# Gate matrices in a transformer block on one Trainium2 core: two products of rounded one-hots in place of one fp32 product, key constants in PSUM, and a contiguous copy of the experts' gate column

## What is computed

```python
q = (xt @ w_q).reshape(T, PEER_HEADS, 2, PEER_HALF)
s = jnp.einsum('thpc,hpnc->thpn', q, sub_keys)
s_top, i_top = lax.top_k(s, PEER_TOPK)
...
best_s, pos = lax.top_k(cand_s, PEER_TOPK)
idx = jnp.take_along_axis(cand_i, pos, axis=-1)
gate = jax.nn.softmax(best_s.astype(jnp.float32), axis=-1).astype(xn.dtype)
...
    act = jax.nn.gelu(jnp.einsum('tkd,td->tk', u_tab[ib], xb), approximate=False)
    return jnp.einsum('tk,tkd->td', act * gb, v_tab[ib])
```

## Time and profile before

| | us |
|---|---|
| median of 3 runs | 1575.96 |
| lowest and highest of the runs | 1575.76, 1586.25 |
| span of the profiled execution | 1581.1 |
| PE busy, DVE busy, ACT busy in that span | 1524.7, 1326.5, 720.5 |
| mean granted TensorE clock | 0.992 of full speed |

### The profile page before, as it was taken

The page is one execution under the profiler, slowest core; times in us unless marked ns, Lnnn a source line. Parts: engine busy times, 40 slices in busy tenths (PEclk is TensorE's granted clock), DMA queues, the critical chain, the costliest instruction groups (busy, mean ns, idle before and its releaser), DMA issues. The chain is left out here.

```text
span 1581.1 us, 24984 instructions
## 1 busy us (share of the span) xinstructions
PE 1524.7 (96%) x9451; PEld 1388.1 (88%) x9451; DVE 1326.5 (84%) x2360; ACT 720.5 (46%) x1442; POOL 339.2 (21%) x301
## 2 busy tenths in 40 slices
PE   7999799999999999999998999999999999999999
PEld 6898688889998999989998999999999888888887
DVE  4638777776799999988974999998989999999996
ACT  4553454141344698788763333333333334333332
POOL 4011620010466100301220222222322211111100
PEclk9999899999999999999999999999999999999999
DMA  5220004031444567878998999999998999999982
GB/s 197 86 81 1 8 29 160 30 111 50 132 165 153 168 196 214 316 241 282 366 366 312 334 360 354 341 352 328 372 339 315 354 407 376 380 363 340 351 290 97
DMA packets 152236, 384.12 MB, mean 243 GB/s; under 512 B 11072, under 2 KB 92096, under 8 KB 135488
## 3 DMA queue, kind: packets, MB, share of 16 engines
q1 hardware_dynamic: 122176, 232.75, 41.9%
q0 software_dynamic: 18432, 134.23, 23.4%
q10 hardware_dynamic: 11520, 15.73, 2.7%
HBM read 337.58 MB, written 45.09 MB: 242 GB/s over the span
## 5 line engine op out<-in xcount | busy, mean ns | idle before, releaser
L1795 POOL DMA_INDIRECT scores<-in_peer_uv,pair_index x86 | 126.2, 1468 | 620.2 <-DVE pair_sum L1819 503.2
L1984 PE MATMUL bank<-x_hi,u_split 128*128 128x384 f32 x640 | 220.3, 344 | 10.6 <-POOL u_split L1919 5.5
L1986 PE MATMUL bank<-x_hi,u_split 128*128 128x384 f32 x640 | 215.8, 337 | 0.0
L1985 PE MATMUL bank<-x_lo,u_split 128*128 128x384 f32 x640 | 215.6, 337 | 0.0
L2273 PE MATMUL bank<-v_hi,act_hi 128*128 128x512 f32 x528 | 206.2, 391 | 1.0 <-DVE v_lo L2336 1.0
L2275 PE MATMUL bank<-v_hi,act_lo 128*128 128x512 f32 x528 | 205.9, 390 | 0.0
L2274 PE MATMUL bank<-v_lo,act_hi 128*128 128x512 f32 x528 | 205.7, 390 | 0.0
L2352 DVE TENSOR_TENSOR act_tile<-gelu_tile,onehots 128x384 f32<-128x384 f32 x128 | 118.2, 923 | 43.8 <-ACT gelu_tile L2321 33.1
L2310 ACT ACTIVATE act_hi<-act_tile 128x384 fp32r<-128x384 f32 x128 | 66.6, 521 | 182.0 <-PE bank L2275 130.9
L1984 PEld LDWEIGHTS bank<-x_hi,u_split 128*128 128x128 f32 x640 | 121.0, 189 | 13.0 <-issue 5.9
L2261 PE MATMUL bank<-x_hi,u_split 128*128 128x384 f32 x384 | 129.1, 336 | 1.4 <-PEq L1929 1.4
(11 more groups left out here) (325 smaller groups left out, 3625.0 us busy)
## 6 DMA issues: line engine op xcount, KB each, us to landing
v_raw<-in_peer_v SPq DMA_DIRECT2D x128, 512.0 KB
u_raw<-in_peer_u SPq DMA_DIRECT2D x64, 512.0 KB, 7.0
u_raw_more<-in_peer_u SPq DMA_DIRECT2D x64, 512.0 KB, 6.7
gates<-gate_stage SPq DMA_DIRECT2D x24, 1024.0 KB, 6.0
onehots<-gates SPq DMA_DIRECT2D x32, 768.0 KB, 8.9
early_gelus<-early_gelu ACTq DMA_DIRECT2D x80, 192.0 KB
gelu_tile<-early_gelus SPq DMA_DIRECT2D x80, 192.0 KB
w_raw<-in_w_in SPq DMA_DIRECT2D x9, 1024.0 KB, 5.2
```

What stands on the lines that cost most here:

```text
L1795: pool.indirect_dma_start(self.slot(k), None, self.table, bass.IndirectOffsetOnAxis(ap=self.sidx[:, k:k + 1], axis=0)).then_inc(self.lande ...
L1984: nc.tensor.matmul(banks.bank(g)[:, 0:TD], uh[:, q, w], m.xh[:, k, P:], start=(k == 0), stop=False)
L1985: nc.tensor.matmul(banks.bank(g)[:, 0:TD], uh[:, q, w], m.xl[:, k, P:], start=False, stop=False)
L1986: t = nc.tensor.matmul(banks.bank(g)[:, 0:TD], ul[:, q, w], m.xh[:, k, P:], start=False, stop=(k == KD - 1))
```

## The change

Four edits, in `Selection`, `routing` and `experts`.

1. The plain one-hots `oj` and the gated ones `og` become fp32r tiles, and each token's gate matrix is the sum of two products: `og`, whose scale is the gate and which is rounded on the way out, and a new tile `ogl`, whose scale is the gate minus its rounded value (`smallT[:, :, 3]`, made once per block by two small DVE instructions). ACT builds both, so `gated` issues 16 instructions a batch. The rings become 2 (`oi`, `og`, `ogl`) and 3 (`oj`).
2. `iota`, `row0` and `step` move to PSUM bank 7, by `place_constants`. The routing stage hands out 7 banks.
3. In `experts` ACT first copies the gate column to a contiguous `act_tile` (`copy_gate`), of which there are now two, and DVE multiplies the gelu into it in place.
4. `load_gates` waits for the copies in place of the multiplications.

```diff
@@ class Selection
-        self.iota = mem.take("rt_iota_row", [P, NK])
+        self.iota_made = mem.take("rt_iota_row", [P, NK])
...
-        self.step = part_of("index_steps", [P, 2, PH, TOPK])
...
+    def place_constants(self, dve, bank):
+
+        link = self.link(dve)
+        self.iota, self.row0 = bank[:, 0:NK], bank[:, NK:NK + TOPK]
+        self.step = bank[:, 256:512].rearrange("p (q h a) -> p q h a", q=2, h=PH)
+        link(self.nc.vector.tensor_copy(self.iota, self.iota_made[:]))
+        link(self.nc.vector.tensor_copy(self.row0, self.row0_made[:]))
@@ def routing
+    og_lo_ready = sem("rt_onehot_gated_low")
+    banks = Banks(ps[:7], done, {"act": sem("rt_by_act"), "dve": sem("rt_by_dve")})
...
-    RING = 3
+    RI, RJ, RG = 2, 3, 2
...
-        oj = m.mem.over("onehot_j", [P, RING, BT, NK], "onehots")
-        oi = m.mem.over("onehot_i", [P, RING, BT, NK], "onehots", F32, 4 * RING * BT * NK)
-        og = sb("onehot_gated", [P, RING, BT, NK])
-        smallT = sb("rt_smallT", [P, 2, 3, P])
+        oj = m.mem.over("onehot_j", [P, RJ, BT, NK], "onehots", F32R)
+        oi = m.mem.over("onehot_i", [P, RI, BT, NK], "onehots", F32, 4 * RJ * BT * NK)
+        og = sb("onehot_gated", [P, RG, BT, NK], F32R)
+        ogl = [m.mem.over("onehot_gated_low0", [P, BT, NK], "onehots", F32R, 4 * (RJ + RI) * BT * NK),
+               sb("onehot_gated_low1", [P, BT, NK], F32R)]
+        smallT = sb("rt_smallT", [P, 2, 4, P])
...
+                        pe.wait_ge(og_lo_ready, BT // 4 * n + i + 1)
                         for q in range(4):
-                            t = nc.tensor.matmul(banks.bank(g)[:, q * NK:(q + 1) * NK],
-                                                 og[:, slot(b, k), 4 * i + q, :], oj[:, slot(b, k), 4 * i + q, :],
-                                                 start=True, stop=True)
+                            out, t = banks.bank(g)[:, q * NK:(q + 1) * NK], 4 * i + q
+                            nc.tensor.matmul(out, og[:, n % RG, t, :], oj[:, n % RJ, t, :], start=True, stop=False)
+                            t = nc.tensor.matmul(out, ogl[n % RG][:, t, :], oj[:, n % RJ, t, :], start=False, stop=True)
...
                     act.wait_ge(oi_ready, n + 1)
-                    wait_products(act, n)
+                    wait_products(act, n - RG)
                     for t in range(BT):
-                        ins = nc.scalar.activation(og[:, slot(b, k), t, :], oi[:, slot(b, k), t, :], ACT.Copy,
+                        ins = nc.scalar.activation(og[:, n % RG, t, :], oi[:, n % RI, t, :], ACT.Copy,
                                                    scale=smallT[:, b % 2, 1, k * BT + t:k * BT + t + 1])
+                        low = nc.scalar.activation(ogl[n % RG][:, t, :], oi[:, n % RI, t, :], ACT.Copy,
+                                                   scale=smallT[:, b % 2, 3, k * BT + t:k * BT + t + 1])
...
                     banks.wait_taken(dve, ("small", b))
+                    link = sel.link(dve)
+                    link(nc.vector.tensor_copy(gate_hi[:], smallT[:, b % 2, 1]))
+                    link(nc.vector.tensor_tensor(smallT[:, b % 2, 3], smallT[:, b % 2, 1], gate_hi[:].bitcast(F32),
+                                                 ALU.subtract))
...
                 early_low(0)
+                sel.place_constants(dve, ps[7])
@@ def experts
-        af = m.mem.over("act_tile", [P, TD], "early_gelu")
+        af = [m.mem.over("act_tile0", [P, TD], "early_gelu"), m.mem.take("act_tile1", [P, TD], at_end=True)]
...
+                def copy_gate(n):
+                    it, jj = n // BODY, n % BODY
+                    if jj == 0:
+                        act.wait_ge(g_in[it % 2], 32 * (it // 2 + 1))
+                    if n >= 2:
+                        act.wait_ge(gated, n - 1)
+                    else:
+                        act.wait_ge(nxt.ge_out[n], 16 * (EARLY // 2))
+                    nc.scalar.activation(af[n % 2][:], gt[:, it % 2, :, jj], ACT.Copy).then_inc(gate_cols, 1)
+
                 split_u(1)
+                copy_gate(0)
...
+                    if n + 1 < NK:
+                        copy_gate(n + 1)
                     if n + 2 < NMT:
                         split_u(n + 2)
...
-                    nc.vector.tensor_tensor(af[:], ge[n % NG2][:], gt[:, it % 2, :, jj], ALU.mult).then_inc(gate_f, 1)
+                    dve.wait_ge(gate_cols, n + 1)
+                    nc.vector.tensor_tensor(af[n % 2][:], ge[n % NG2][:], af[n % 2][:], ALU.mult).then_inc(gate_f, 1)
```

More of the change, by code:

```diff
@@ L1332, in __init__ @@
         self.zsum = part_of("rt_z", [P, PH])
-        self.row0 = part_of("row_starts", [P, TOPK])
+        self.row0_made = part_of("row_starts", [P, TOPK])
         self.rowd = part_of("row_lengths", [P, TOPK])
@@ L1861, in routing @@
     stored = [sem("gates_out0"), sem("gates_out1")]
-    banks = Banks(ps, done, {"act": sem("rt_by_act"), "dve": sem("rt_by_dve")})
+    og_lo_ready = sem("rt_onehot_gated_low")
+    banks = Banks(ps[:7], done, {"act": sem("rt_by_act"), "dve": sem("rt_by_dve")})
     BT = 8
     NBT = P // BT
-    RING = 3
+    RI, RJ, RG = 2, 3, 2
     ST = 16
@@ L1908, in routing @@
         stage = sb("gate_stage", [P, 2, NK // GJ, ST, GJ])
-        oj = m.mem.over("onehot_j", [P, RING, BT, NK], "onehots")
-        oi = m.mem.over("onehot_i", [P, RING, BT, NK], "onehots", F32, 4 * RING * BT * NK)
-        og = sb("onehot_gated", [P, RING, BT, NK])
-        smallT = sb("rt_smallT", [P, 2, 3, P])
-        small, iota = sel.small, sel.iota
+        oj = m.mem.over("onehot_j", [P, RJ, BT, NK], "onehots", F32R)
[4 more added lines that the diff above has]
+        smallT = sb("rt_smallT", [P, 2, 4, P])
+        gate_hi = sb("rt_gate_hi", [P, P], F32R)
+        small = sel.small
         u_raw = m.u_raw
@@ L1919, in u_low @@
             return on.tensor_tensor(ul[:, n % 2, :], u_raw[n % NU], uh[:, n % 2, :].bitcast(F32), ALU.subtract)
-        def slot(b, k):
-            return (NBT * (b - 1) + k) % RING
         def wait_products(eng, n):
-            if n >= RING:
-                banks.wait_full(eng, ("G",) + BATCHES[n - RING] + (BT // 4 - 1,))
+            if n >= 0:
+                banks.wait_full(eng, ("G",) + BATCHES[n] + (BT // 4 - 1,))
         with nc.Block() as block:
@@ L1996, in pairs @@
                     t.then_inc(done, 1)
-                keep_turning(nc, m, banks.banks[7], 18)
+                keep_turning(nc, m, banks.banks[6], 18)
                 for n in range(FIRST):
@@ L2102, in one_hot @@
                     return nc.vector.tensor_tensor(
-                        out[:, slot(b, k)], iota[:].unsqueeze(1).broadcast_to([P, BT, NK]),
+                        out, sel.iota.unsqueeze(1).broadcast_to([P, BT, NK]),
                         smallT[:, b % 2, q, k * BT:(k + 1) * BT].unsqueeze(2).broadcast_to([P, BT, NK]), ALU.is_equal)
@@ L2114, in first_keys @@
                 def first_keys(n):
-                    if n >= RING:
-                        dve.wait_ge(og_ready, BT // 4 * (n - RING + 1))
-                    one_hot(oi, n, 0).then_inc(oi_ready, 1)
+                    if n >= RI:
+                        dve.wait_ge(og_ready, BT // 4 * (n - RI + 1))
+                        dve.wait_ge(og_lo_ready, BT // 4 * (n - RI + 1))
+                    one_hot(oi[:, n % RI], n, 0).then_inc(oi_ready, 1)
                 early_low(0)
+                sel.place_constants(dve, ps[7])
                 sel.link(dve)(nc.vector.memset(pairs_of_0.sums[:], 0.0))
@@ L2131, in _ @@
                         first_keys(n + 1)
-                    wait_products(dve, n)
-                    one_hot(oj, n, 2).then_inc(oj_ready, 1)
+                    wait_products(dve, n - RJ)
+                    one_hot(oj[:, n % RJ], n, 2).then_inc(oj_ready, 1)
                     early_low(early(n) + 1)
@@ L2203, in load_gates @@
                     if it >= 2:
-                        sp.wait_ge(gate_f, (it - 1) * BODY)
+                        sp.wait_ge(gate_cols, (it - 1) * BODY)
                     v = slice(half * TD // 2, (half + 1) * TD // 2)
@@ L2309, in split_act @@
                         act.wait_ge(down_done, n - NA + 1)
-                    nc.scalar.activation(ah[:, n % NA, :], af[:], ACT.Copy).then_inc(gate_hi, 1)
+                    nc.scalar.activation(ah[:, n % NA, :], af[n % 2][:], ACT.Copy).then_inc(gate_hi, 1)
+                def copy_gate(n):
[7 more added lines that the diff above has]
+                    nc.scalar.activation(af[n % 2][:], gt[:, it % 2, :, jj], ACT.Copy).then_inc(gate_cols, 1)
                 split_u(1)
+                copy_gate(0)
                 for n in range(NK + 1):
@@ L2343, in gate @@
                         dve.wait_ge(ge_in[n % NG2], 16 * ((n - NMT) // NG2 + 1))
-                    it, jj = n // BODY, n % BODY
-                    if jj == 0:
-                        dve.wait_ge(g_in[it % 2], 32 * (it // 2 + 1))
-                    if n:
-                        dve.wait_ge(gated, n)
```

(8 more changed lines are left out.)

11 lines of the change are left out of this document (7 added, 4 removed).

## The result

The kernel after takes 1727.3 us (median of three runs, 1727.1 to 1729.1), before 1575.96. The ratio is 1.0949, with an interval of 1.0917 to 1.0981: slower by 151 us, where the forecast was 116 and its range ended at +144.

The account below looks back on a forecast made before the run. PE was taken to set the pace everywhere before the change. Routing +64.5 us, last part +47.5 and mixed part +4 summed to +116 on the 1576 us median, 1692 us; range 1655 to 1720.

Parts of the forecast that it names:

- constants in PSUM: Before the batches: PE's waits for POOL's work on u go, as DVE collides less with it; -5.5 us, bounds 0 and 5.5.
- batches: Gate batches: ACT's eight extra instructions make rounds 7.51 us in place of 5.16; 367 us against 294, +73 us.
- behind the batches: After the last batch: PE's 3.05 us wait for a low part of u goes, as DMAs have more room; -3 us.
- mixed part: Mixed part: rounds of 8.41 us against PE's 8.25 over 46 iterations, 7 us at most; +4 us taken.
- last part: Last part: rounds of 4.76 us against PE's 4.13; 377.8 us against 330.3, +47.5 us.
- The bounds on the fp32r product: Gate batches: an fp32r product of 128 columns costs PE between 0.06 and 0.224 us; 0.112 taken.
- D: Experts: time of ACT's strided copy of one gate column; 0.84 us taken, 0.52 if the stride costs nothing.
- the signs of being wrong: PE above 97% busy in either stretch, a copy under 0.6 us, or batch rounds under 7.3 or over 7.8 us.
- the forecast's own average: Mixed part: the round between ACT and DVE averages 7.57 us plus the copy's time, 8.41 against PE's 8.25.
- the closed round: Experts: `act_lo`, copy, `v_hi`, `v_lo`, pair step, next `act_lo`, without PE; 4.76 us in the last part against PE's 4.13.
- 25 us lower: Experts: how much the sum falls if ACT's strided copy runs at one element per cycle, whatever the stride.
- the rival's +86.5: Experts: rival in which ACT reads the gate column at full speed, 0.52 us; +86.5 us, 1662 us, chance 0.17.

Follow-up runs that it names:

- second profile of before: The unchanged kernel before, profiled once more to check the first profile's span; its span is 1574.9 us, 6.2 less, and its median 1576.6 us.
- psum_and_copy_behind: The kernel before with the selection's constants in PSUM, seven routing banks, and the experts' gate copy placed behind `v_hi`; no second one-hot; 1571.0 us, ratio 0.9956.
- Three_tiles: The kernel after with three `act_tile` in turn, so the copy waits for `act_lo` of n-2 in place of n-1; 1651.3 us, ratio 1.0458.
- copy_contiguous: The kernel after with ACT's copy reading 384 contiguous elements in place of every eighth, so the gates are wrong numbers; 1675.2 us, ratio 1.0616.
- copy_behind: The kernel after with the gate copy moved behind `split_v(n - 1)` in ACT's order, nothing left out; 1646.2 us, ratio 1.0433.

## Why the prediction was right and wrong

Against the second profile of before, the 152.5 us between the ends divide like this:

| step | forecast | measured |
|---|---|---|
| constants in PSUM | -5.5 | -7.2 |
| batches | +73 | +79.3 |
| behind the batches | -3 | -1.1 |
| mixed part | +4 | +21.3 |
| last part | +47.5 | +60.3 |

**Right.** ACT's in-order queue sets the batches, at 7.5 us per round as forecast. The copy closes a round between ACT and DVE in which PE has no part. Both halves were shown: without the eight low copies the 79 us of the batches go, and with the copy behind `v_hi`, or with a third tile, the last part returns to PE's 326 us. The bounds on the fp32r product were wide, and the value taken, 0.112 us, is what the rows show; the reason given for it (weights as many and as wide) was not tested, so that is in part luck. That DVE's saved 0.37 us per column are worth nothing is shown by psum_and_copy_behind.

**Wrong: D.** "I take 0.84, as DVE's is the only strided read of this very tile" is the step that failed. ACT's strided copy takes 0.97 us. I had charged the stride with ACT's own 0.82 ns per element once more, 0.32 us; it costs ACT 0.45 (DVE 0.37, which would have been too little as well). D stands in every round, so in the last part 79 x 0.13 = 10 us are from it, and about 6 in the mixed part. I gave the range an end below 0.84 and none above, and so it was with the signs of being wrong: none of them came true (PE 87 and 89% busy, a copy over 0.6 us, rounds of 7.5 us). D alone would have taken the forecast to about 1708 us, so it isn't the whole miss.

**Wrong: the mixed part.** "46 iterations give 7 us at most; PE has some room at the start, so I take 4." It cost 21.3. With D = 0.97 the forecast's own average is 7.57 + 0.97 = 8.54 against PE's 8.25. Measured, 44 rounds are 8.57 us and cost 13.9 us in all; so the closed round is right here too, and PE had no room that took anything off. The other 7.5 us, which the sum didn't have, lie at the two ends. PE's waits in after, before the first down and at the passage to the last part:

```profile
929.81 0.47 PE L2293 MATMUL bank<-v_hi,act_hi 128*128 128x512 f32 x1 [1.51 <-DVE v_lo L2369]
...
1321.35 0.47 PE L2293 MATMUL bank<-v_hi,act_hi 128*128 128x512 f32 x1 [1.98 <-DVE v_lo L2369]
...
1328.64 0.47 PE L2293 MATMUL bank<-v_hi,act_hi 128*128 128x512 f32 x1 [2.92 <-DVE v_lo L2369]
```

The first costs 1.7 us: the fourth up comes 10.03 us after the third, for 8.36 before. From the last up to column 48 it is 23.5 us for 17.7, which is 5.8: the waits ahead of columns 46 and 47 are 3.9 us longer in all than before, and behind the wait of 2.92 the down of column 47 runs at a lower granted clock, 5.8 us for 4.16. Three_tiles loses 1.7 and 3.1 us at the same places, 1.6 of them by the clock again, copy_contiguous 0.7 and 2.6, copy_behind nothing. So both come with the copy's place ahead of `v_hi`. I read it as the two places where PE has no columns in hand; no run isolates that. Rounds with four pair steps in place of three cost nothing by themselves: copy_contiguous has them, and its ups stay 8.25 us apart.

**Wrong: a column.** The row at 1244.23 is the down of column 47, not 48: in that profile `v_hi_late` is first read at 1248.4. The 330.3 us were 81 columns, 4.08 us each, and the forecast set 80 against them. That is 4 us.

**Wrong: the batches' edges, and one wait.** The sum had 48 rounds of 7.51 us. The first, which has nothing to evict yet, takes 4.69, and the last takes 10.6, from 884.64 to the end; the two nearly cancel. The larger part is one wait of ACT of 4.2 us, which its own round doesn't have:

```profile
666.99 16.48 SPq L1945 DMA_DIRECT2D u_raw<-in_peer_u  x1
...
690.38 1.06 ACT L2039 ACTIVATE u_split<-u_raw 128x1024 fp32r<-128x1024 f32 x1 [4.17 <-PE bank L1994]
```

The profile names PE, but the load of this very u, whose issue takes SP 16.48 us, lands at 690.31 by the trace. The kernel before waits there as well, and no engine is named:

```profile
652.08 14.35 SPq L1937 DMA_DIRECT2D u_raw_more<-in_peer_u  x1
...
673.65 1.06 ACT L2030 ACTIVATE u_split<-u_raw_more 128x1024 fp32r<-128x1024 f32 x1 [4.61 <-issue]
```

**Wrong: one execution.** The first profile of before is 6.2 us longer than the second: 1.9 in the batches (294.2 for 292.2) and 4.3 behind them, where I took off 3 us that only such an execution has. The forecast's own sum had noted 5.1 us between that profile's span and the median. After, span and median agree, so those 5 us were part of the rise of the medians and not of the sum.

**Smaller.** The constants gave 7.2 us, more than the 5.5 set as their upper end. That end was the sum of PE's listed waits; four ups that hold such a wait take 5.5 to 5.9 us in place of 4.16, 6.2 us in all, and some shorter gaps go too. The sentence that puts the sum "25 us lower" for a read at full speed leaves out the 4 us of the mixed part; the rival's +86.5 has them.

In all the forecast was short by 35 us and its range by 7. D and the mixed part's ends and average make up 28 of them, and D's 16 alone are more than the range missed by.

## What to carry to other kernels

Work moved to an idle engine is paid for by where it stands in that engine's order, and by what it waits for. The same 0.97 us copy cost 81 us ahead of `v_hi` and nothing behind it; before adding a wait to an in-order engine, list what is queued behind it and who waits for that. A number that enters each round of a closed loop needs both ends of its range, and a difference between profiled span and median should be looked for in a second profile before any term rests on a wait seen once. An edit of three parts is to be timed in parts: here one part was a gain of 0.7%, and the other two hid it under 10%. And where the profile says for whom an engine waited, the landing of the load that it also needs should be looked at.
